# A hybrid sequence model on one core: the split products with their columns in reverse order

## The reference

```python
h = rms_norm(x); x = x + mixer(h @ w_in) @ w_out      # gated delta rule + SSD; stick-breaking; gated linear attention
h = rms_norm(x); u = causal_dwconv(h @ w_up)          # w_up 1024 x 5632, three taps
gate, up = split(u); x = x + (silu(gate) * up) @ w_down   # w_down 2816 x 1024
```

## Time and profile before

| | us |
|---|---|
| median of 3 runs | 2150.36 |
| lowest and highest of them | 2149.61, 2154.43 |
| the profiled execution, whole | 2149.57 |
| its span, first to last instruction | 2147.8 |
| TensorE busy in the span | 2098.5 |
| VectorE, ScalarE, GpSimd busy | 1212.0, 906.0, 326.6 |

### The profile page before, as it was taken

How to read it: one execution, slowest core, us unless ns; L and a number is a source line. 1 busy time by engine, 2 the same in 40 slices (tenths; PEclk the granted TensorE clock), 3 DMA queues, 4 the chain that set the end, 5 groups by cost and what they waited for, 6 DMA issues and landing times.

```text
span 2147.8 us, 26841 instructions
## 1 busy us (share of the span) xinstructions
PE 2098.5 (98%) x9776; PEld 1699.6 (79%) x9776; DVE 1212.0 (56%) x1663; ACT 906.0 (42%) x1282; POOL 326.6 (15%) x266
## 2 busy tenths in 40 slices
PE   6999999999999999999999999999999999999999
PEld 4778888878868888887766888888868878888887
DVE  5898755765366666225544566653354465666522
ACT  5883445434244444224564444442242354444411
POOL 0001221220112222001301122220000012222200
PEclk9999999999999999999999999999999999999999
DMA  7323222122212223222211232332222122222321
GB/s 235 94 75 96 82 77 71 49 69 73 95 67 94 93 96 120 95 82 67 69 40 49 89 98 98 98 114 94 86 69 88 60 73 94 98 98 97 115 95 66
DMA packets 81481, 188.96 MB, mean 88 GB/s; under 512 B 19824, under 2 KB 40432, under 8 KB 81392
## 3 DMA queue, kind: packets, MB, share of 16 engines
q1 hardware_dynamic: 81392, 187.75, 26.9%
HBM read 178.28 MB, written 9.44 MB: 87 GB/s over the span
## 4 chain that ended last, share of the span: by engine, by line
PE 92%; DVE 4%; ACT 2%; issue 1%; DMA 0%; POOL 0%; SPq 0%; DVEq 0%; ACTq 0%
PE acc L256 23%; PE acc L258 23%; PE acc L257 23%; PE bank L1248 1%; PE bank L232 1%; PE bank L1730 1%; PE bank L234 1%; PE bank L233 1%; PE acc L2636 1%; PE acc L2637 1%; PE acc L2638 1%; PE bank L2021 1%; PE bank L256 1%; PE bank L258 1%; PE bank L257 1%
## 5 line engine op out<-in xcount | busy, mean ns | idle before, releaser
L256 PE MATMUL acc<-HH,whi 128*128 128x512 f32 x1600 | 644.1, 403 | 6.8 <-DVE wlo L194 4.3
L258 PE MATMUL acc<-HH,wlo 128*128 128x512 f32 x1600 | 626.2, 391 | 0.0
L257 PE MATMUL acc<-HL,whi 128*128 128x512 f32 x1600 | 625.3, 391 | 0.0
L188 ACT ACTIVATE whi<-raw 128x1024 fp32r<-128x1024 f32 (+1 forms) x293 | 324.1, 1107 | 567.0 <-PE acc L258 537.7
L194 DVE TENSOR_TENSOR wlo<-raw,whi 128x1024 fp32r<-128x1024 f32 (+1 forms) x293 | 399.7, 1365 | 283.3 <-ACT whi L188 283.3
L256 PEld LDWEIGHTS acc<-HH,whi 128*128 128x128 f32 x1600 | 302.1, 189 | 73.8 <-DVE wlo L194 9.5
L258 PEld LDWEIGHTS acc<-HH,wlo 128*128 128x128 f32 x1600 | 301.5, 188 | 64.8
L257 PEld LDWEIGHTS acc<-HL,whi 128*128 128x128 f32 x1600 | 302.3, 189 | 62.5 <-issue 4.1
L256 PE MATMUL acc<-FH,whi 128*128 128x512 f32 x528 | 205.8, 390 | 0.0
L257 PE MATMUL acc<-FL,whi 128*128 128x512 f32 x528 | 205.4, 389 | 0.0
L258 PE MATMUL acc<-FH,wlo 128*128 128x512 f32 x528 | 205.4, 389 | 0.0
(11 more groups left out here) (393 smaller groups left out, 2666.8 us busy)
## 6 DMA issues: line engine op xcount, KB each, us to landing
raw<-w SPq DMA_DIRECT2D x257, 512.0 KB, 3.5
raw<-w SPq DMA_DIRECT2D x48, 704.0 KB, 3.9
X<-x SPq DMA_DIRECT2D x4, 512.0 KB, 5.4
x_dram<-small SPq DMA_DIRECT2D x8, 256.0 KB, 4.3
xt_dram<-small SPq DMA_DIRECT2D x8, 256.0 KB, 3.7
a_dram<-l_am SPq DMA_DIRECT2D x8, 256.0 KB, 3.4
l_xt<-xt_dram SPq DMA_DIRECT2D x8, 256.0 KB, 3.3
l_x<-x_dram SPq DMA_DIRECT2D x8, 256.0 KB, 3.2
```

Of the source, the lines that this page charges most:

```text
L188: nc.scalar.activation(hi[:, 0:kt * P], raw[u % RAW][:, 0:kt * P], ACT.Copy).then_inc(w_hi_ready, 1)
L256: nc.tensor.matmul(a[:, :], wh, tile(hi, k), start=start and k == 0, stop=False)
L257: nc.tensor.matmul(a[:, :], wh, tile(lo, k), start=False, stop=False)
L258: last = nc.tensor.matmul(a[:, :], wl, tile(hi, k), start=False, stop=stop and k == kt - 1)
```

## The change

A helper `back(t, k)` gives tile k of `t` as a view with step -1: element 511 first, element 0 last. All split products use it for the moving operand and for the accumulator. So a product's first streamed column is frame 511, and its sum goes to column 511 of the accumulator; each column's sum ends where it did before. The weights, the instructions and their number, the semaphores, all other engines, the plain products and the filler products stay as they are.

```diff
+        def back(t, k=0):
+            return t[:, (k + 1) * S - 1:k * S - 1 if k else None:-1]
...
-                nc.tensor.matmul(a[:, :], wh, tile(hi, k), start=start and k == 0, stop=False)
-                nc.tensor.matmul(a[:, :], wh, tile(lo, k), start=False, stop=False)
-                last = nc.tensor.matmul(a[:, :], wl, tile(hi, k), start=False, stop=stop and k == kt - 1)
+                nc.tensor.matmul(back(a), wh, back(hi, k), start=start and k == 0, stop=False)
+                nc.tensor.matmul(back(a), wh, back(lo, k), start=False, stop=False)
+                last = nc.tensor.matmul(back(a), wl, back(hi, k), start=False, stop=stop and k == kt - 1)
```

More of the change, by code:

```diff
@@ L231, in fan @@
                     a, (wh, wl) = c["spare"][j], (x[:, k * P:(k + 1) * P] for x in w[j])
-                    nc.tensor.matmul(a[:, :], wh, tile(hi, k), start=k == 0, stop=False)
-                    nc.tensor.matmul(a[:, :], wh, tile(lo, k), start=False, stop=False)
-                    last = nc.tensor.matmul(a[:, :], wl, tile(hi, k), start=False, stop=k == KD - 1)
+                    nc.tensor.matmul(back(a), wh, back(hi, k), start=k == 0, stop=False)
+                    nc.tensor.matmul(back(a), wh, back(lo, k), start=False, stop=False)
+                    last = nc.tensor.matmul(back(a), wl, back(hi, k), start=False, stop=k == KD - 1)
                     if k == KD - 1:
@@ L1467, in begin_pe @@
                         pe.wait_ge(w_lo_ready, m + 1)
-                    nc.tensor.matmul(a[:, :], wh, tile(HH, k), start=k == 0, stop=False)
-                    nc.tensor.matmul(a[:, :], wh, tile(HL, k), start=False, stop=False)
-                    last = nc.tensor.matmul(a[:, :], wl, tile(HH, k), start=False, stop=k == KD - 1)
+                    nc.tensor.matmul(back(a), wh, back(HH, k), start=k == 0, stop=False)
+                    nc.tensor.matmul(back(a), wh, back(HL, k), start=False, stop=False)
+                    last = nc.tensor.matmul(back(a), wl, back(HH, k), start=False, stop=k == KD - 1)
                     if k == KD - 1:
@@ L2635, in mix_pe @@
                     wh, wl = whi[w][:, j * P:(j + 1) * P], wlo[w][:, j * P:(j + 1) * P]
-                    nc.tensor.matmul(a[:, :], wh, tile(hi, j), start=h == 0 and j == 0, stop=False)
-                    nc.tensor.matmul(a[:, :], wh, tile(lo, j), start=False, stop=False)
-                    last = nc.tensor.matmul(a[:, :], wl, tile(hi, j), start=False, stop=h == 1 and j == KD - 1)
+                    nc.tensor.matmul(back(a), wh, back(hi, j), start=h == 0 and j == 0, stop=False)
+                    nc.tensor.matmul(back(a), wh, back(lo, j), start=False, stop=False)
+                    last = nc.tensor.matmul(back(a), wl, back(hi, j), start=False, stop=h == 1 and j == KD - 1)
                 last.then_inc(unit_done, 1)
```

## The result

The changed kernel takes 2191.98 us in the median of 4 runs (2191.91 to 2195.55), and the kernel before 2150.79 us in the median of 4. The ratio is 1.0193, with a 95% interval of 1.0175 to 1.0210: slower by 41 us. The forecast was 2150 us and no difference. The time is inside the stated range, but between the two places at which I expected it.

The account below looks back on a forecast made before the run. TensorE was taken as the bound, 7752 products 0.2267 us apart; all terms of the change were 0, so 2149.57 us profiled, with a median of 2150.36, gave 2150 us. The range was 2145 to 3716 us.

Parts of the forecast that it names:

- the two places at which I expected it: Whole kernel's time: 2150 us with no difference (chance 0.60), or about 3700 us with products at half rate (0.27).
- What bounds the kernel: TensorE throughout: time is the sum of distances between its instructions' starts, 7752 products at 0.2267 us, 1757 us.
- The helper and the issue: Building the reversed views: each product stays one instruction with its own weight load, count 9776; cost 0.
- the hand-overs: Waits between engines: readers wait for a product's completion, TensorE for whole tiles, so column order doesn't matter; cost 0.
- The write of the sums: Products' writes into PSUM: reversed columns touch the same neighbours, so the distance stays 0.2267 us; cost 0.
- the streaming of the moving operand: TensorE's read in every split product: reversed columns touch the same neighbours, distance stays 0.2267 us; cost 0.
- half rate: Every split product: reversed read or write takes one column per 1.2 GHz cycle, 0.2000 us more, about 3700 us; chance 0.27.
- my two ends: Bounds for the distance of a reversed product: 0.2154 us as a gain, 0.4288 us as half rate.
- small fixed price per product: Start of each reversed stream: 0.001 to 0.0044 us more, 8 to 34 us in all, 2170 us; chance 0.07.

Follow-up runs that it names:

- sum_only_down: Changed kernel with the moving operand read front to back again, only the sums written back to front: 2149.85 us, ratio 1.000 to the kernel before.
- read_only_down: Changed kernel with the sums written front to back again, only the moving operand read back to front: 2193.02 us, ratio 1.0195 to the kernel before.
- first kernel of streams: Separate kernel, 32 products per variant without waits, varying order, width and type: fp32r at 512 columns 0.2269 us between starts up, 0.2334 down.

## Why the prediction was wrong

**What bounds the kernel** was read rightly: TensorE's distances, 7752 products at 0.2267 us. A loss of 0.0067 us in each product of a settled stream came through to the end.

**The helper and the issue, and the hand-overs**, costed at 0, were right: the count is 9776, and the chain is TensorE's as before. The write of the sums was right too. `sum_only_down` shows it at 0 within 0.12%.

**The step that failed is the streaming of the moving operand**, which the sum had at 0. I took 0.2267 us, because a reversed stream touches the same neighbours. The fp32r read at full rate is not indifferent to the order. What was measured is 0.2333 us, and `read_only_down` has the whole of it. That the time lies inside the range is luck, since the range reached beyond 2184 us only for the sake of half rate. The value lay between my two ends (0.2154 and 0.4288 us), but I gave the middle to nothing: "between about 2190 and 3680 I expect almost nothing", and the time stands at the edge of that stretch.

**The rival "small fixed price per product"** named the right kind of loss and mis-sized its term. It had 0.001 to 0.0044 us, taken from how much one instruction varies with what surrounds it. Those were two means of nine gaps. Single gaps in the same unit run from 0.224 to 0.236 us, and its first is 0.316, so nothing made 0.0044 an upper bound, and the price was 0.0067. It isn't fixed either: it is 0.0044 us at 384 columns, nothing at 320 and below zero at 256.

**Half rate** fell by a factor of 30 in the price. The two rows that I took for it are of streams which are slow for other reasons than the order. Plain float32 is at 0.429 us up and down (lines 98 and 100). And in the first kernel of streams too, rising products begin 0.427 us apart (the second to the ninth gap of its first line) and come to 0.2267 with their order unchanged. Why the start is slow the profiles don't say. I also misread: a plain float32 product is two instructions in the trace (64 for the 32 products of line 98), so those eight were four products of 0.86 us. The distance between instructions, which the bound used, was right.

**Working the sum again.** Both traces have a mark ahead of the second layer's feed-forward part, the product of line 354 (358 after), and the same mark again ahead of the third layer's mixer. Before:

```profile
1203.17 1.02 PE L354 MATMUL bank<-sq,cst 128*128 128x512 f32 x2
...
1563.96 1.02 PE L354 MATMUL bank<-sq,cst 128*128 128x512 f32 x2
```

After:

```profile
1221.29 1.02 PE L358 MATMUL bank<-sq,cst 128*128 128x512 f32 x2
...
1592.61 0.59 PE L358 MATMUL bank<-sq,cst 128*128 128x512 f32 x1
```

From mark to mark it was 360.79 us and is 371.32: 10.5 us more. Between them lie the 44 units of w_up and the 16 of w_down, 44 x 24 + 16 x 33 = 1584 products, and 1584 x 0.0067 = 10.6. Over the whole kernel 7752 x 0.0067 would be 51.9 us, and 42.4 are seen. The two traces hold the same 9776 instructions in the same order, so each gap can be set beside its partner:

| gaps | number | change, us | each, us |
|---|---|---|---|
| between split products, settled (ten or more behind a break) | 6198 | +41.0 | +0.0066 |
| between split products, nearer behind a break | 1163 | +3.8 | +0.0033 |
| between split products, over 0.3 us in either trace | 226 | -3.8 | -0.017 |
| before or behind a plain or a filler product | 2188 | +1.7 | +0.0008 |

The sum is 42.7 us from TensorE's first start to its last. So the settled products pay in full, those shortly behind a break pay half, and the long gaps pay nothing. These long ones are the first gaps behind a break, waits for another engine, and the start at half rate, which ended sooner after than before. More than half of the products close behind a break stand in the first mixer. For its 1248 input products the first two classes give 4.5 us and not 8.3, and 4.5 is inside the interval of 0.6 to 5.2 that was measured.

**On the two rules of the Trainium skill.** The one on PSUM (PSUM — Partial Sum Buffer, "Specifications (TRN2)"), that a non-contiguous pattern slows matmuls, doesn't reach a reversed one: sums written down cost 0 here. The one on SBUF (SBUF — State Buffer, "Door 1: The DMA port swizzle"), full bandwidth while consecutive accesses share a line of 16 bytes, would make the reversed read free. The measured 0.0067 us and the ratio of 1.0195 of `read_only_down` decide against it for falling fp32r columns at this width, and line 151 against it for every second column, which also has two in each 16 bytes: 256 such columns take 0.2263 us, as long as 512 neighbours (0.2267) and nearly twice the 0.1200 of 256.

**What stays open** is the mechanism inside the reader. The runs show where the order matters at 512 columns, above 16 bytes and below 256, and that of the three types tried it matters for fp32r alone (bf16 has 2-byte columns, plain float32 runs at half the rate). They don't show what the reader does with such a piece, nor why the price changes with the width as it does. Nor did any order tried beat rising order at 512 columns: no version came out that would beat the kernel before.

## What to carry to other kernels

Where TensorE streams are the bound, a moving operand of 512 fp32r columns wants rising order in runs of at least 64 columns; the order of the runs, and the order of the sums, is free. A change that leaves every count and wait alone can still cost 2%, because 0.0067 us times 7752 is 52 us, of which 42 showed, so an unknown in the cost of the commonest instruction wants a continuous range and not two points. A price measured in a settled stream is, in the mean, too much for products shortly behind a break, which are slower already (0.0033 us here in place of 0.0067).

## What the runs showed of the hardware

- The price of falling order in the fp32r moving read is 0.0067 us at 512 columns, 0.0038 at 448, 0.0044 at 384, none at 320 (both 0.1466 us), and a gain of 0.0019 at 256 (0.1181 against 0.1200). With 16-column pieces turned round inside rising order it is 0.040 us (0.2666 against 0.2266).
- Every second column of an fp32r moving operand halves the rate: 0.2263 us for 256 columns, as for 512 neighbours.
- Behind a break, rising products are at first 0.2306 us apart (mean of the 1163 gaps under 0.3 us that are among the first nine) and then 0.2267; reversed ones are at 0.2339 and then 0.2333. The first gap of all is longer, 0.316 us in the unit shown.
- A rising fp32r read that starts at column 32 of a tile is slower than one from column 0, by 0.0029 us at 384 columns and 0.0009 at 448.
